# Two linears of branch C's output gate moved from between the key units to between the value units

## The reference

```python
# per layer
h = rmsnorm(x)
z = h @ w_in                      # one projection, 1024 -> 6320 columns
                                  # ... gg is 512 of its columns: branch C's output gate
# branch A, sample tokens: 32 cached pages of 128 positions for each of 8 sequences
s_past = q_lat @ ckv_past.T + q_rope @ kr_past.T      # key pages are read
pr     = softmax(concat([s_past, s_new]) * scale)
o_lat  = pr @ ckv_past                                # value pages are read
# branch C: gated linear attention
h_c = rmsnorm(o, g_gla) * silu(gg)
# merge
mix = sum_j sigmoid(gate_j) * (branch_j @ w_p_j)
x = x + mix @ w_o ; x = x + swiglu(rmsnorm(x))
```

## Time and profile before

| | |
|---|---|
| median of 3 runs | 2142.83 us (2136.88 to 2144.74) |
| the profiled execution's own time | 2133.87 us |
| its span | 2132.2 us |
| TensorE busy | 2054.4 us, 96% |
| VectorE, ScalarE, GpSimd busy | 49%, 34%, 14% |
| DMA, mean over the span | 151 GB/s |
| mean granted TensorE clock | 0.987 of 2.4 GHz |

### The profile page before, as it was taken

One profiled execution on the slowest core, in us unless ns is written; L12 is line 12 of the kernel. 1 busy time (PEld: TensorE's weight loads), 2 busy tenths in 40 slices (PEclk: granted clock), 3 DMA queues, 4 the chain that ended last, 5 costly groups with the idle time before them and its releaser, 6 DMA issues.

```text
span 2132.2 us, 50002 instructions
## 1 busy us (share of the span) xinstructions
PE 2054.4 (96%) x21088; PEld 1936.2 (91%) x21088; DVE 1035.3 (49%) x1590; ACT 719.1 (34%) x1133; POOL 298.1 (14%) x534
## 2 busy tenths in 40 slices
PE   8999999999999999999999999998999999999997
PEld 7887878788999999999998888786899999999997
DVE  6666523246746444443357654133566554444323
ACT  4444214146334322222234431142553332222221
POOL 0102455520000000000001034555000000000000
PEclk9999999999999999999999999999999999999999
DMA  5226899973333333333342378999523323333332
GB/s 211 73 57 194 291 330 320 314 237 91 103 91 106 92 90 90 94 90 92 92 142 83 93 236 291 327 328 321 166 67 121 110 84 95 90 91 98 89 93 68
DMA packets 164534, 322.45 MB, mean 151 GB/s; under 512 B 24419, under 2 KB 102806, under 8 KB 163798
## 3 DMA queue, kind: packets, MB, share of 16 engines
q10 hardware_dynamic: 46944, 147.87, 22.9%
q1 hardware_dynamic: 92790, 100.04, 14.4%
q0 software_dynamic: 24576, 71.34, 9.9%
HBM read 307.08 MB, written 12.08 MB: 150 GB/s over the span
## 4 chain that ended last, share of the span: by engine, by line
PE 79%; DVE 8%; DMA 5%; issue 3%; ACT 3%; SPq 1%; ACTq 0%; POOLq 0%; POOL 0%; DVEq 0%
PE PS L1755 23%; PE PS L1757 23%; PE PS L1756 23%; DMA kpg<-in_cache_keys 3%; DMA vpg<-in_cache_vals 2%; PE PS L2000 2%; DVE wl L682 2%; PE PS L2030 2%; PE PS L1808 1%; PE PS L2005 1%; PE PS L1794 1%; SPq L2365 1%; ACT P L1432 1%; DVE P L847 1%; ACT wh L1336 1%
## 5 line engine op out<-in xcount | busy, mean ns | idle before, releaser
L1755 PE MATMUL PS<-hh,wh 128*128 128x260 f32 x3008 | 866.8, 288 | 8.1 <-DVE wl L682 5.5
L1757 PE MATMUL PS<-hl,wh 128*128 128x260 f32 x3008 | 854.2, 284 | 0.0
L1756 PE MATMUL PS<-hh,wl 128*128 128x260 f32 x3008 | 853.2, 284 | 0.0
L1755 PEld LDWEIGHTS PS<-hh,wh 128*128 128x128 f32 x3008 | 571.1, 190 | 23.4 <-issue 14.0
L1757 PEld LDWEIGHTS PS<-hl,wh 128*128 128x128 f32 x3008 | 571.3, 190 | 0.0
L1756 PEld LDWEIGHTS PS<-hh,wl 128*128 128x128 f32 x3008 | 571.0, 190 | 0.2
L682 DVE TENSOR_TENSOR wl<-raw,wh 128x1024 fp32r<-128x1024 f32 (+4 forms) x326 | 359.5, 1103 | 322.4 <-ACT wh L1336 321.8
L1336 ACT ACTIVATE wh<-raw 128x1024 fp32r<-128x1024 f32 (+4 forms) x326 | 304.6, 937 | 456.2 <-PE PS L1757 455.4
L1755 PE MATMUL PS<-fh,wh 128*128 128x260 f32 x704 | 198.9, 283 | 0.0
L1757 PE MATMUL PS<-fl,wh 128*128 128x260 f32 x704 | 198.7, 282 | 0.0
L1756 PE MATMUL PS<-fh,wl 128*128 128x260 f32 x704 | 198.6, 282 | 0.0
(11 more groups left out here) (330 smaller groups left out, 2986.5 us busy)
## 6 DMA issues: line engine op xcount, KB each, us to landing
raw<-in_wpack ACTq DMA_DIRECT2D x238, 512.0 KB, 3.6
kpg<-in_cache_keys SPq DMA_DIRECT2D x256, 144.0 KB, 4.3
vpg<-in_cache_vals SPq DMA_DIRECT2D x256, 128.0 KB, 5.7
vpg<-in_cache_vals POOLq DMA_DIRECT2D x256, 128.0 KB, 5.5
kpg<-in_cache_keys POOLq DMA_DIRECT2D x208, 144.0 KB, 4.0
raw<-in_wpack ACTq DMA_DIRECT2D x48, 256.0 KB, 3.0
raw<-in_wpack ACTq DMA_DIRECT2D x16, 384.0 KB, 3.2
kx_most<-in_cache_keys POOLq DMA_DIRECT2D x42, 144.0 KB, 3.7
```

The costliest lines, as they stand in the source:

```text
L1755: pe.matmul(out, w[0], x[0], start=first, stop=False)
L1756: pe.matmul(out, w[1], x[0], start=False, stop=False)
L1757: return pe.matmul(out, w[0], x[1], start=False, stop=last)
```

## The change

Two of the four gate blocks, `gg10` and `gg11`, leave the list of fillers of the key stage. Ten fillers are left, each with three key units. The two linears now stand in the value stage, behind the gates `g13` (round 2) and `g16` (round 5). Their evacuation on VectorE, their slab conversions and their Silu move with them.

```diff
-KEY_FILLERS = ("gg00", "gg01", "gq0", "gk0", "gv00", "gv01", "gq1", "gk1", "gv10", "gv11", "gg10", "gg11")
+KEY_FILLERS = ("gg00", "gg01", "gq0", "gk0", "gv00", "gv01", "gq1", "gk1", "gv10", "gv11")
 KEYS_FIRST = 2
-KEY_STEPS = [(2, 5, 7) if n % 2 == 1 else (3, 7) for n in range(len(KEY_FILLERS))]
+KEY_STEPS = [(2, 5, 7)] * len(KEY_FILLERS)
+VALUE_FILLERS = {2: "gg10", 5: "gg11"}
...
         lin(f"g1{c + 1}" if c < 7 else "g00")
+        if c in VALUE_FILLERS:
+            lin(VALUE_FILLERS[c])
...
                     if c:
                         gate(1, c)
+                    if c - 1 in VALUE_FILLERS:
+                        name = VALUE_FILLERS[c - 1]
+                        dve.wait_ge(*upto(f"pe {name}"))
+                        dve.tensor_tensor(halves(sgs[int(name[2])][:, int(name[3]), :]), pair(name), halves(rs[:, :]), ALU.mult).then_inc(*mark("dve_evac", f"free {name}"))
...
                     weights(si[f"g1{c + 1}" if c < 7 else "g00"])
+                    if c in VALUE_FILLERS:
+                        weights(si[VALUE_FILLERS[c]])
...
+                    if c in VALUE_FILLERS:
+                        weights(si[VALUE_FILLERS[c]])
                     if c < 7:
                         gate(1, c + 1)
+                    if c in VALUE_FILLERS:
+                        branch_c(VALUE_FILLERS[c])
...
                         linear(f"g1{c + 1}", [f"g1{c + 1}"], hh, hl)
+                        if c in VALUE_FILLERS:
+                            linear(VALUE_FILLERS[c], [VALUE_FILLERS[c]], hh, hl)
```

## The result

The changed kernel takes 2156.11 us (median of 20 runs, 2140.38 to 2166.94) against 2137.23 us of the kernel before on the same chips (20 runs, 2128.55 to 2144.74). The ratio is 1.0073 with a 95% interval of 1.0059 to 1.0087: by it some 16 us **slower** (19 by the two medians), where 8 us faster were forecast, and above the top of the range, 2146. The profiled execution of after took 2156.73 us with a span of 2155.0 and a mean granted clock of 0.982, against 2133.87, 2132.2 and 0.987.

A forecast was written before the change was run, and what follows sets the result against it. TensorE's work was taken to set the time, except where it waits for key and value pages. Wins of 5.0 us in layer 1 and 3.3 in layer 2 made 8.3: 2142.8 to 2134.5 us, range 2124 to 2146.

The forecast's parts named there:

- The value stage: the step that failed: Value stages: each added linear gives the loads 5.87 us, less 1.6 for its slab, so 4.3 us of cover.
- 1.4 + 0.8 us: Value stages of layers 1 and 2: TensorE waits expected to stay, out of the present 6.86 and 7.63 us.
- The slower rival: Value stage: linear and block hold TensorE 11.8 us without freeing a slot, DMA runs dry; 2153 us, 10 lost; chance 0.06.
- The key stage: Becomes bound by page loads; TensorE stalls at unit 31 grow to 8.7 and 8.6 us from 5.66 and 5.07.
- 328 GB/s: Key stage: load rate at DMA share 0.99, by which a filler's 4.06 MB take 12.4 us against TensorE's 10.7.
- the closed gap: DMA gap behind the mixing, 6.7 and 6.3 us: 1.4 us stay, 5.3 and 4.9 are won.
- the gap only moves: Lower bound for the DMA gap behind the key stage's mixing: 0 us won.
- the queue's delay: Key stage, fetch of unit 17: 1.9 us, taken from unit 15's issue, within some 10 us of waiting for unit 14.
- the third case: Key stage: key pages load at the value pages' 355 GB/s; 19 us won, 2124 us; chance 0.04.
- 2.6 us were to be won: Layer 1's value stage: slow clock after waits costs 1.5 and 1.1 us; the clock is kept after the change.
- The other engines' part: Value stage: moved evacuation, Silu, conversions and table loads cost nothing; 3 to 6 us per layer if cover were gone.
- the signs listed as wrong: Low DMA share behind gg10 or gg11, key-stage idle over 12 us, waits for wl or evacuations, longer waits after the value stage.

The follow-up runs named there:

- experiment 5: Kernel before with all 30 key units packed into the first ten fillers, gg10 and gg11 behind them without units: 2155.78 against 2139.95 us, ratio 1.0065.
- experiment 3: Changed kernel with gg10 and gg11 moved behind P13 and P16, into the middle of rounds 3 and 6: 2142.84 us, ratio 1.0009 to the kernel before.
- the split: Kernel before with each key unit's pages issued half by SyncE's and half by GpSimd's queue, in reading order: 2125.88 us, ratio 0.9937.
- the split and spread kernel: Kernel before with key units issued over two queues and each round's units 8c+6 and 8c+7 inside the gate's linear: 2112.88 us, ratio 0.9882.

## Why the prediction was wrong

**The value stage: the step that failed.** "A linear added there gives the loads 5.87 us and takes 1.6 us for its own slab: 4.3 us of cover." It took the late landings for late bytes that any work ahead of them makes good. The waits are between the first and the last unit of one round, and the linears were put between two rounds. 1.4 + 0.8 us were forecast to stay; 11.2 + 8.1 did, all but the 2.40 of round 1 at the last unit of a round. That is 17 of the 31 us between the forecast for the profiled execution (2125.6) and what it took (2156.73); some 11 more are clock, 2 are key waits. The rows that told it were among those shown: the waits of the earlier trace rows come some 16 us apart, one round, each in front of the last eight matmuls of one, in both layers. A late start of the loads would have shown at the first units of a round as well, where the trace of before has only 0.29, 0.30 and 1.10 us, at the end of a first half.

**The slower rival saw why the cover failed**, and where: the linear and the block behind it free no slot for 11.8 us, the DMA runs dry. The share of 0.50 and 0.38 over `gg10` and `gg11` and GpSimd's 8.17 and 11.25 us of nothing are its signs, named in advance. It had 0.06. But its price was not the one it named, 10 us against the kernel before: by experiment 5 the place between the rounds costs 2 us against a place ahead of the stage, which is within the noise, and the loss against the kernel before comes from the packing, 13.9 of 16 us. What the place did cost is the cover that it didn't give: 14 us by experiment 3, against the middle of the rounds. So that its time of 2153 came near the measured one is luck.

**The key stage: the number right by luck, the reason not.** 8.7 and 8.6 us of waits were forecast, 9.6 and 9.9 measured. But they were derived from a landing of unit 31 set by 328 GB/s, less 5 us for the closed gap. The gap didn't close: 5.3 and 4.9 us were taken, some 1 came in each layer (6.7 us of idle over 240 to 280 in the earlier trace rows and its neighbours before, 6.0 after; 6.4 and 5.2 in layer 2). Its bound of 0, "the gap only moves", was nearly the truth: units 15 and 16 were fetched early, as said, but unit 18 waited for unit 15, and so every third unit down the stage (21, 24, 27). The landing of unit 31 came at 330.4 and not at 325.7, 4.7 us later; that the wait is only 0.9 us longer than forecast comes from a second error, which hid the first: at half clock TensorE itself needed some 3.5 us more to get there. 1.9 us for "the queue's delay" was the time to the *first* issue of a unit; the last of its eight is under way until 4.65 us after that, and this was left out.

**The rate.** 328 GB/s was read as the engines' limit for key pages because the share was 0.99. With the split the same pages run at 346 over 70 us and at 363 over ten. So the third case, key pages at 355 GB/s, was right about the hardware, and at 0.04 too lightly put aside; the changed kernel asked for less, 306 GB/s from 260 to 330. The Trainium skill, "DMA: Bandwidth & Descriptors", section "Specifications", puts the limit of one core at about 358 GB/s; the stretches of 363, and of 374 from 360 to 370 in the kernel before, lie above it by up to 5%. The same page, section "Issuing engines are not separate DMA queues", says that starting DMAs on several engines only saves the sequencers' time, "which is usually small relative to the DMA itself". Here it isn't: 4.65 us of eight issues stand against 4.0 to 4.5 us from an issue to its landing, and splitting them over two queues, in the order of reading, was worth 13 us.

**The clock.** 2.6 us were to be won, 8 were lost: PEclk 0.96 in three of the four stretches. It was held for a by-product of the waits, which was right, but its sign went with theirs. Of the clock alone the moved linears made one thing worse: in layer 1 the 13.1 us from 434.82 for two linears that take 11.7, behind the wait of 1.99.

**What held.** The work taken out and put in, 11.6 to 11.7 us per layer, closes the ledger within 1 us. The other engines' part (evacuation, Silu, table loads, later decays) cost nothing that can be seen: no wait of TensorE for `wl` or for an evacuation in rounds 3 and 6. Of the signs listed as wrong, the low share at the linears came; so did linears of 7 us and more (7.4 from 417.91), which were to be absent; the key waits stayed under 12 us per layer.

## What to carry to other kernels

Before counting a moved piece of work as cover for a late load, find the instruction that released the slot of that load, and put the work between that release and the need; work ahead of the release covers little (5 of 23.5 us here, 12 in the middle of the rounds) and holds up the releases behind it. A DMA share of 0.99 says that the engines had something to do, not that they could do no more: where a ring has few slots, count from the release to the *last* issue of the refill and its landing, and try the issues split over two queues. And packing the consumers of a ring of three more densely shortens that window for every unit, which here cost 14 us with no work added.

## What was unexpected of the hardware

- Eight page DMAs of 144 KB take 4.65 us of a queue's time to issue, 0.58 each, and land 4.0 to 4.5 us after issue in the median. From a freed slot to a landed unit it is 9.5 to 12.4 us.
- The same 1.18 MB units, the same 16 engines: 326 GB/s at share 0.99 with each unit on one queue, 346 at 1.03 with each on two (and in the order of reading).
- Waits of nearly one length have unlike sequels. After 2.74 us at 417.34 the next linear takes 7.4 us, after 2.80 at 457.72 it takes 5.9, after 1.99 at 434.25 it is slow again. What decides it isn't in these rows. The clock fell where TensorE had just waited, and not each time.
- A gap of the DMA of 6 of ten microseconds (share 0.42) in front of 80 us at full load cost TensorE nothing in layer 1 of the split and spread kernel, where no key page was late.
